# RWKV key factors: the sums one projection tile later, one square root ahead of the next eviction, and the spread to channels by sixteen 32-row products over four banks

## The chip, the cores and the metric

One core of one Trainium2 chip runs the whole program. The metric is device time in microseconds (us), the median of several executions. The engines are named as in the profile: PE (TensorE, matrix products), PEld (its weight loads), DVE (VectorE), ACT (ScalarE), POOL (GpSimd) and SP (SyncE, which here only issues transfers).

## The reference, cut to what matters

The program is a decoder trunk of two layers over 512 tokens with a model width of 1024. Each layer projects the normed tokens once (`proj = h @ w_in`), feeds three mixers with the parts of that product, projects back, attends to a memory and ends in a mixture of 32 experts. The change lies in one step of the RWKV mixer, which has 8 heads of 64 channels:

```python
kk = k * k_k.astype(f32).reshape(H, N)
kk = kk / jnp.maximum(jnp.sqrt(jnp.sum(kk * kk, axis=-1, keepdims=True)), 1e-12)
y = rwkv7_scan(r, decay, k, v, -kk, kk * a)
```

For every token and head the squares of the 64 channels of `kk` are summed, the reciprocal root of the sum is a factor, and all 64 channels are multiplied by it. There are 512 tokens by 8 heads of such factors in a layer.

## The kernel before, in words

Everything lies transposed: channels on the 128 partitions, tokens along the free dimension. The 512 RWKV channels of a quantity are four blocks c = 0 to 3 of 128 channels (two heads each). All data is f32, and a matrix product shows in the profile as two PE instructions (passes): eight products of a tile are 16 passes.

The stage around the change is the input projection (lines 708 to 1077). PE computes 19 tiles of 128 channels by 512 tokens, in the order `TILE_ORDER` (line 45), which is here called tile 0 to tile 18. A tile is eight products over the model width (line 1063), accumulated in one of the four PSUM banks B[0] to B[3] in turn. Before tile n PE waits until the bank's last tile has been evicted (`s_pad`). After each tile it looks in a table written by hand, `between` (line 1054), for other work to put in: `kk_sums` after tile 8, `kk_spread` after tile 10, `early_a` after tile 13. PE executes its instructions in this order, so whatever a `between` step waits for also holds up the next tile.

ACT evicts each tile (`evict(n)`, lines 774 to 784, copies at 782 or 784), DVE then mixes it with the tokens shifted by one (`shift(m)`, lines 871 to 880), where `shift(7)`, `shift(8)`, `shift(9)` belong to tiles 8, 9 and 10. Both engines also work in the order of the code.

The key factors go through all engines:

- DVE scales the keys into `X1` (line 906); ACT squares `X1` into `kk_sq` (line 830), between the evictions of tile 8 and tile 9.
- PE, `kk_sums` (line 998): `heads_summed` multiplies with `head_pick`, four blocks of 32 output rows for each c, so that rows 32i to 32i+31 of B[4], columns 0 to 127, hold the sums of head rows for the 128 tokens of token tile i. These are 16 products, 32 passes (line 287).
- DVE (lines 917 to 919), after `shift(8)`: floor at 1e-24 and reciprocal into `hf`, 128 x 128.
- POOL (line 762) has zeroed `kk_rs`, 128 x 512, after waiting for the sums. ACT (line 835), after `evict(10)`: `root_by_tile` takes the root of each 32-row band i of `hf` into columns 128i to 128i+127 of that band of `kk_rs` (four instructions, line 299), so that the other bands of these columns stay zero.
- PE, `kk_spread` (line 1003): `heads_given` multiplies the 128 x 128 matrix `head_give[:, c, :]` with `kk_rs`, one product of 512 columns for each c into B[4] to B[7] (line 293, eight passes in all).
- DVE (lines 921 to 923), after `shift(9)`: multiplies `X1[:, c, :]` with B[4 + c], each c as soon as its product is there. After tile 11 (`V_DONE`) it goes on with the decays and with A and B, which `early_a` needs (lines 925 to 938).

Each 32-row band of `head_give` holds the same pattern, written by POOL at the start of the stage (lines 755 to 760). The function `heads_given` and `root_by_tile` are used a second time later in the layer, in a stage that the change doesn't touch. After the stage come the recurrence, the output projection, the memory attention and the experts, whose weights SP loads into a ring of SBUF units as PE releases them (line 1979).

Of the kernel before, what the change touches and what calls it, by code (L numbers as in the profile page):

```python
# [9 lines left out]
ACT = mybir.ActivationFunctionType  # L10
# [3 lines left out]
P = 128  # L14
DEPTH, SEQ, D = 2, 512, 1024
NT = SEQ // P
KD = D // P
MEM = 256
RC = 4
# [52 lines left out]
def build(nc, xT_d, memT_d, pos_d, inv_d, colp_d, memcol_d, w_in_d, lora_d, gup_d, gup2_d, wuq_d, wukv_d, wsT_d,  # L72
          gb_d, w_out_d, wkv_d, wm_d, wr_d, br_d, we_d, out_d):
    ctx = ExitStack()
    with ctx:
# [15 lines left out]
        def sb(name, shape, dt=F32):  # L91
            return ctx.enter_context(nc.sbuf_tensor(name, shape, dt))
# [4 lines left out]
        def sem(name):  # L97
            stage.append(held[0].enter_context(nc.semaphore(name)))
            return stage[-1]
# [52 lines left out]
        B = [banks[:, i, :] for i in range(8)]  # L152
# [4 lines left out]
        ring = sb("ring", [P, 6, 4096])  # L157
# [47 lines left out]
        def in_chunks(ap):  # L205
            return ap.rearrange("p (q t) -> p q t", t=C)
# [74 lines left out]
        head_give = ring[:, 5, 1536:2048].rearrange("p (c n) -> p c n", c=RC)  # L281
# [9 lines left out]
        def heads_given(bank, c, src):  # L291

            return nc.tensor.matmul(bank[:, :], head_give[:, c, :], src, start=True, stop=True)

        def root_by_tile(eng, out, src):

            for i in range(NT):
                rows = slice(32 * i, 32 * i + 32)
                last = eng.activation(out[rows, i * P:(i + 1) * P], src[rows, :], ACT.Sqrt)
            return last  # L300
# [50 lines left out]
        def rows_landed(eng, done):  # L351
            eng.wait_ge(s_yo[0], 16 * (NE // 2) * done)
            eng.wait_ge(s_yo[1], 16 * (NE // 2) * done - 16)
            eng.wait_ge(s_yl, 32)
            if done == DEPTH:
                eng.wait_ge(s_yx, 32)
# [285 lines left out]
        for layer in range(DEPTH):  # L642
# [19 lines left out]
            for c in range(RC):  # L662
# [11 lines left out]
            s_b1, s_b2, s_b3 = sem("kk_squared"), sem("kk_summed"), sem("kk_floored")  # L674
            s_b4, s_b5 = sem("kk_root"), sem("lora_tanh")
            s_b6, s_b7, s_b8 = sem("kk_factors"), sem("kk_factors_spread"), sem("gate_tanh")
            s_kn = sem("kk_normed")
            hf, kk_rs = ring[:, 5, 2048:2048 + P], ring[:, 5, 3072:3584]
            s_hg, s_kz = sem("head_give_ready"), sem("kk_factors_zeroed")
            s_wp, s_ap, s_th, s_ta = sem("decay_lora"), sem("a_lora"), sem("decay_tanh"), sem("a_tanh")  # L680
            s_cr, s_ex, s_bp, s_bs = (sem("cum_ready"), sem("decay_exps"), sem("bonus_product"),
                                            sem("bonus_summed"))
# [8 lines left out]
            def flat(ap):  # L691
                return ap.rearrange("p c t -> p (c t)")
# [4 lines left out]
            NTILE = len(TILE_ORDER)  # L697
# [10 lines left out]
            with nc.Block() as block:  # L708
# [38 lines left out]
                @block.gpsimd  # L747
                def _(eng):
                    g = gch.on(eng)
                    if layer:  # L750
                        rows_landed(eng, layer)
                        combine_gather(eng, ys_d[0:NE * CAP, :])
                        scale_first(eng, layer)
                    g(eng.memset(shp[:, :, 0:1], 0.0))
                    g(eng.memset(head_give[:, :, :], 0.0))
                    for i in range(NT):
                        v = head_give[:, :, :].rearrange("p c (e n) -> p c e n", e=2)
                        g(eng.affine_select(out=v, in_=v, compare_op=ALU.not_equal, fill=1.0, base=-32 * i,
                                            pattern=[[-2, RC], [-1, 2], [0, RN]], channel_multiplier=1))
                    eng.sem_inc(s_hg, 1)  # L760
                    eng.wait_ge(s_bs, 1)
                    eng.memset(kk_rs, 0.0).then_inc(s_kz, 1)

                    eng.wait_ge(s_ai, 16)
                    g(eng.affine_select(out=l_blk, in_=a_blk, compare_op=ALU.is_gt, fill=0.0, base=0,
                                        pattern=[[1, 32], [-1, 32]], channel_multiplier=0))
                    eng.affine_select(out=l_blk, in_=l_blk, compare_op=ALU.not_equal, fill=1.0, base=0,
                                      pattern=[[1, 32], [-1, 32]], channel_multiplier=0).then_inc(s_bm, 1)

                @block.scalar  # L770
                def _(eng):
                    a = ach.on(eng)

                    def evict(n):
                        j = TILE_ORDER[n]
                        _, w, _, shifted = TILE[j]
                        eng.wait_ge(s_pj, n + 1)
                        if shifted:
                            m = sum(TILE[x][3] for x in TILE_ORDER[:n])
                            if m >= 2:  # L780
                                eng.wait_ge(s_sh, m - 1)
                            eng.activation(shp[:, m % 2, 1:SEQ + 1], B[n % 4][:, :], ACT.Copy).then_inc(s_pad, 1)  # L782
                        else:
                            eng.activation(dest[j][0:w, :], B[n % 4][0:w, :], ACT.Copy).then_inc(s_pad, 1)
# [29 lines left out]
                    for z in range(2):  # L814
                        for n in range(2):
                            c = 2 * z + n
# [12 lines left out]
                        eng.wait_ge(s_yz, 16)  # L829
                    eng.activation(flat(kk_sq), flat(X1), ACT.Square).then_inc(s_b2, 1)  # L830
                    evict(9)
                    evict(10)
                    eng.wait_ge(s_b3, 1)
                    eng.wait_ge(s_kz, 1)
                    root_by_tile(eng, kk_rs, hf).then_inc(s_b4, 1)
                    evict(11)
                    eng.wait_ge(s_cr, 1)
                    eng.activation(flat(X6), flat(X6), ACT.Exp).then_inc(s_ex, 1)
# [28 lines left out]
                def _(eng):  # L867
# [3 lines left out]
                    def shift(m):  # L871
                        n, j = order[m]
                        eng.wait_ge(s_pad, n + 1)
                        v(eng.tensor_tensor(shd[:, :], shp[:, m % 2, 0:SEQ], shp[:, m % 2, 1:SEQ + 1],  # L874
                                            ALU.subtract))
                        out = dest[j] if 4 <= j < 12 else in_chunks(dest[j])
                        eng.scalar_tensor_tensor(out=out, in0=in_chunks(shd[:, :]), scalar=col("mu", j),
                                                 in1=in_chunks(shp[:, m % 2, 1:SEQ + 1]), op0=ALU.mult,
                                                 op1=ALU.add).then_inc(s_sh, 1)
                        eng.wait_ge(s_sh, m + 1)  # L880
# [37 lines left out]
                    v(eng.tensor_scalar(hf, B[4][:, 0:P], 1e-24, None, ALU.max))  # L918
                    eng.reciprocal(hf, hf).then_inc(s_b3, 1)
                    shift(9)  # L920
                    for c in range(RC):
                        eng.wait_ge(s_b7, c + 1)
                        last = eng.tensor_tensor(X1[:, c, :], X1[:, c, :], B[4 + c][:, :], ALU.mult)
                    last.then_inc(s_kn, 1)
                    eng.wait_ge(s_pj, V_DONE)
# [53 lines left out]
                def _(eng):  # L979
                    def lora_pair(z):  # L980
                        if z == 0:
                            if not layer:
                                eng.wait_ge(s_kd, 2)
                            eng.wait_ge(s_par, 16 * NPAR * (layer + 1))
                            eng.wait_ge(s_sh, 1)
                            eng.wait_ge(s_b5, 1)
                        for n in range(2):
                            c, cols = 2 * z + n, slice((2 * z + n) * P, (2 * z + n + 1) * P)
                            if z:
                                eng.wait_ge(s_ta, n + 1)  # L990
                            nc.tensor.matmul(B[4 + 2 * n][:, :], lora_w[64:128, cols], lora[64:128, :],
                                             start=True, stop=True).then_inc(s_ap, 1)
                            if z:
                                eng.wait_ge(s_th, n + 1)
                            nc.tensor.matmul(B[5 + 2 * n][:, :], lora_w[0:64, cols], lora[0:64, :], start=True,
                                             stop=True).then_inc(s_wp, 1)
# [6 lines left out]
                    def kk_spread():  # L1003
                        eng.wait_ge(s_hg, 1)
                        eng.wait_ge(s_b4, 1)
                        for c in range(RC):
                            heads_given(B[4 + c], c, kk_rs).then_inc(s_b7, 1)

                    def early_a():
                        eng.wait_ge(s_ab, 2)  # L1010
# [40 lines left out]
                    else:  # L1051
                        nc.tensor.matmul(B[3][:, :], ones_mean[:, :], xsum, start=True, stop=True).then_inc(s_x0, 1)
                    first_products(2, KD).then_inc(s_pj, 1)
                    between = {5: lambda: lora_pair(0), 6: lambda: lora_pair(1), 8: kk_sums, 10: kk_spread, 13: early_a, NTILE + 1: bonus_sums}
                    for n, j in list(enumerate(TILE_ORDER))[1:]:
                        u0, w, unit, _s = TILE[j]
                        eng.wait_ge(s_win[unit], 16 * layer + 16)
# [2 lines left out]
                        for k in range(KD):  # L1060
                            if n == 1:
                                eng.wait_ge(s_h, k + 1)
                            last = nc.tensor.matmul(B[n % 4][0:w, :], ins_units[unit][:, k, u0:u0 + w], hT[:, k, :],  # L1063
                                                    start=k == 0, stop=k == KD - 1)
# [1929 lines left out]
```

## Time and profile before

| | |
|---|---|
| median of 3 runs | 1871.53 us (1870.42 to 1873.68) |
| the profiled execution: its own time | 1873.28 us |
| its span, first to last instruction | 1871.5 us |
| mean granted TensorE clock | 0.985 |
| PE busy | 1755.2 us, 94% of the span |
| DVE busy | 612.2 us, 33% |
| ACT busy | 386.5 us, 21% |
| POOL busy | 182.4 us, 10% |
| hardware DMA queue q1 | 475.45 MB, 62.2% of 16 engines' span |

The profile is of one execution. Starts are counted from the first instruction. "Busy" counts an engine's own instructions; the bracket behind a row of the timeline gives the idle time of that engine just before it and what ended it.
### The profile page before, as it was taken

What the parts mean: (1) busy time and instruction counts of PE and PEld (TensorE: products, weight loads), DVE (VectorE), ACT (ScalarE), POOL (GpSimd) and SP (SyncE); (2) the same over time, 40 slices, a digit from 0 to 9 for tenths busy, and PEclk for the clock granted to TensorE, in tenths of its full rate; (3) what the DMA queues carried; (4) which work ended last, traced back from release to release, by engine and by line L of the source; (5) the groups of instructions that cost most, each with busy time, mean ns of one, the idle gap of its engine ahead of it and who ended that gap; (6) DMA issues with size and microseconds to landing.
All of it is one profiled execution on the core that took longest, in us unless ns stands there. A gap on an engine that the chain in (4) does not pass through costs nothing. (4 is left out here: it accounts for less than half of the span.)

```text
span 1871.5 us, 26294 instructions
## 1 busy us (share of the span) xinstructions
PE 1755.2 (94%) x11146; PEld 866.8 (46%) x11146; DVE 612.2 (33%) x1163; ACT 386.5 (21%) x745; POOL 182.4 (10%) x223
## 2 busy tenths in 40 slices
PE   8989999999999999998699999999999999999985
PEld 6435765455444443433253467545554444333322
DVE  7347554236211111111243574612561111111102
ACT  3131364154000000000212324513510000000001
POOL 3000101004000000000300001000040000000001
PEclk9999999999999999999899999999999999999997
DMA  9502205135999999999850220243279999999996
GB/s 382 208 1 34 37 11 218 57 130 196 405 429 427 427 427 429 428 428 427 313 214 0 34 35 12 81 189 135 91 301 422 427 426 427 427 429 428 427 429 228
DMA packets 90489, 494.83 MB, mean 264 GB/s; under 512 B 45646, under 2 KB 50510, under 8 KB 62736
## 3 DMA queue, kind: packets, MB, share of 16 engines
q1 hardware_dynamic: 82672, 475.45, 62.2%
q0 software_dynamic: 7632, 17.74, 2.6%
q8 instruction: 80, 1.31, 0.3%
q14 instruction: 25, 0.20, 0.0%
q10 hardware_dynamic: 80, 0.13, 0.0%
HBM read 465.34 MB, written 36.18 MB: 268 GB/s over the span
## 5 line engine op out<-in xcount | busy, mean ns | idle before, releaser
L2203 PE MATMUL bank<-ring,hT 128*64 128x512 f32 x2048 | 465.8, 597 | 37.9 <-DMA ring<-in_we 31.7
L2203 PEld LDWEIGHTS bank<-ring,hT 128*64 128x64 f32 x2048 | 139.5, 136 | 313.9 <-issue 250.1
L1063 PE MATMUL bank<-hT,ring 128*128 128x512 f32 (+1 forms) x576 | 250.6, 595 | 0.0
L2211 PE MATMUL bank<-ring,arena 128*64 128x512 f32 x1040 | 236.7, 597 | 11.1 <-DMA ring<-in_we 9.1
L1063 PEld LDWEIGHTS bank<-hT,ring 128*128 128x128 f32 (+1 forms) x576 | 108.3, 189 | 138.8 <-issue 137.5
L2188 PE MATMUL bank<-shift_in,arena 128*128 128x256 bf16 (+1 forms) x1440 | 160.0, 268 | 0.0
L2188 PEld LDWEIGHTS bank<-shift_in,arena 128*128 128x128 bf16 x1440 | 129.9, 98 | 62.7 <-issue 48.7
L2256 DVE TENSOR_TENSOR hT<-bank,colp 128x512 f32<-128x512 f32 (+1 forms) x68 | 45.2, 668 | 340.0 <-PE bank L2188 328.5
L2592 ACT ACTIVATE arena<-bank 128x256 f32<-128x256 f32 x65 | 25.0, 384 | 605.1 <-PE bank L2174 605.1
L2221 POOL DMA_INDIRECT expert_rows<-arena,row_places x63 | 62.1, 986 | 847.3 <-DVE arena L2733 818.9
L2211 PEld LDWEIGHTS bank<-ring,arena 128*64 128x64 f32 x1040 | 71.0, 137 | 143.7 <-issue 126.2
L2733 DVE COPY arena<-bank 128x512 f32<-128x512 f32 x65 | 44.9, 691 | 252.6 <-PE bank L2211 252.2
L2369 PE MATMUL bank<-hT,ring 128*128 128x512 f32 x256 | 110.3, 593 | 2.2 <-PEq L1914 2.2
L2579 ACT ACTIVATE arena<-bank 128x512 f32<-128x512 f32 x65 | 38.9, 598 | 244.4 <-PE bank L2203 244.4
L2705 DVE TENSOR_TENSOR arena<-arena,bank 128x256 f32<-128x256 f32 x65 | 27.4, 421 | 187.6 <-ACT arena L2592 187.4
L2369 PEld LDWEIGHTS bank<-hT,ring 128*128 128x128 f32 x256 | 48.5, 190 | 62.9 <-issue 62.9
L2612 DVE TENSOR_TENSOR xT<-xT,bank 128x512 f32<-128x512 f32 x32 | 22.0, 687 | 138.7 <-PE bank L2369 105.8
L874 DVE TENSOR_TENSOR arena<-shift_in 128x512 f32<-128x512 f32 x30 | 22.1, 736 | 110.6 <-ACT shift_in L782 110.4
L782 ACT ACTIVATE shift_in<-bank 128x512 f32<-128x512 f32 x28 | 16.8, 599 | 178.6 <-PE bank L1063 178.6
L253 ACT ACTIVATE arena<-xT 128x512 f32<-128x512 f32 x32 | 20.2, 630 | 133.5 <-DVE xT L2612 133.5
L2174 PEld LDWEIGHTS bank<-ident,arena 128*128 128x128 f32 x260 | 28.0, 141 | 40.7 <-issue 40.6
L2174 PE MATMUL bank<-ident,arena 128*128 128x128 f32 x260 | 41.9, 284 | 0.0
(464 smaller groups left out, 1884.4 us busy)
## 6 DMA issues: line engine op xcount, KB each, us to landing
ring<-in_we SPq DMA_DIRECT2D x193, 2048.0 KB, 23.6
ring<-in_w_in SPq DMA_DIRECT2D x6, 2048.0 KB, 19.2
expert_rows<-ring SPq DMA_DIRECT2D x1, 8448.0 KB, 25.7
ring<-in_w_out SPq DMA_DIRECT2D x4, 2048.0 KB, 10.1
ring<-in_wm SPq DMA_DIRECT2D x2, 2048.0 KB, 7.3
ring<-in_w_in SPq DMA_DIRECT2D x2, 1920.0 KB, 16.5
ring<-in_w_in SPq DMA_DIRECT2D x2, 1664.0 KB, 27.0
ring<-in_w_in SPq DMA_DIRECT2D x2, 1152.0 KB, 28.7
```

The costliest lines, as they stand in the source:

```text
L1063: last = nc.tensor.matmul(B[n % 4][0:w, :], ins_units[unit][:, k, u0:u0 + w], hT[:, k, :], start=k == 0, stop=k == KD - 1)
L2174: last = nc.tensor.transpose(bank[:, j * P:(j + 1) * P], src[:, j * P:(j + 1) * P], ident[:, :])
L2188: last = nc.tensor.matmul(bank[:, o:o + w], parts[m][:, i, k * P:(k + 1) * P], selg[z][:, i, c0:c0 + w], start=m == 0 and i == 0, stop=m = ...
L2203: last = nc.tensor.matmul(bank[CAP * j:CAP * j + CAP, :], x[:, k, :], ahead_w[4 * j + k] if third else up_w(u, j, k), start=k == 0, stop=k ...
L2211: last = nc.tensor.matmul(bank[CAP * half:CAP * half + CAP, :], hid[u][:, m, :], down_w(slot, m, half), start=m == 0, stop=m == HM - 1)
L2221: eng.indirect_dma_start(out=ys_halves[0:2 * NE * CAP, :], out_offset=bass.IndirectOffsetOnAxis(ap=row_places[:, e:e + 1], axis=0), in_=ys ...
L2256: return eng.tensor_tensor(xgg[z][:, k0:k0 + n, c0:c0 + w], bank[:, 0:n * w].rearrange("p (k s) -> p k s", k=n), gain.unsqueeze(2).to_broa ...
L2369: last = nc.tensor.matmul(B[c % 4][:, :], w_out[:, k, c * P:(c + 1) * P], hT[:, k, :], start=k == 0, stop=k == KD - 1)
L2579: eng.activation(hr[w], b_up[w][:, :], ACT.Copy).then_inc(s_hr, 1)
L2592: eng.activation(sg[w], up_half(b_flip[w], 0), ACT.Silu).then_inc(s_sg, 1)
L2705: eng.tensor_tensor(hid[w], sg[w], up_half(b_flip[w], 1), ALU.mult).then_inc(s_hd, 1)
L2733: eng.tensor_copy(ysb[w], b_down[w][:, :]).then_inc(s_ys, 1)
```

## The change

`kk_sums` moves from after tile 8 to after tile 9. The root becomes one ACT instruction over `hf`, 128 x 128, in place, and moves ahead of `evict(10)`. `kk_rs`, its zeroing on POOL and their semaphore go. `kk_spread`, still after tile 10, becomes 16 products of 32 rows by 128 columns: in round r block c takes token tile i = (c + r) mod 4, so that a round's four products read four different 32-row bands and write four different banks, B[4] to B[7]. Before rounds 1 to 3 PE waits for the completion of its own products of the rounds before. DVE waits for all 16 before its first multiplication with the factors.

```diff
-            hf, kk_rs = ring[:, 5, 2048:2048 + P], ring[:, 5, 3072:3584]
-            s_hg, s_kz = sem("head_give_ready"), sem("kk_factors_zeroed")
+            hf = ring[:, 5, 2048:2048 + P]
+            s_hg = sem("head_give_ready")
@@ gpsimd
                     eng.sem_inc(s_hg, 1)
-                    eng.wait_ge(s_bs, 1)
-                    eng.memset(kk_rs, 0.0).then_inc(s_kz, 1)
-
                     eng.wait_ge(s_ai, 16)
@@ scalar
                     evict(9)
+                    eng.wait_ge(s_b3, 1)
+                    eng.activation(hf, hf, ACT.Sqrt).then_inc(s_b4, 1)
                     evict(10)
-                    eng.wait_ge(s_b3, 1)
-                    eng.wait_ge(s_kz, 1)
-                    root_by_tile(eng, kk_rs, hf).then_inc(s_b4, 1)
                     evict(11)
@@ vector
                     shift(9)
+                    eng.wait_ge(s_b7, RC * NT)
                     for c in range(RC):
-                        eng.wait_ge(s_b7, c + 1)
                         last = eng.tensor_tensor(X1[:, c, :], X1[:, c, :], B[4 + c][:, :], ALU.mult)
@@ tensor
                     def kk_spread():
                         eng.wait_ge(s_hg, 1)
                         eng.wait_ge(s_b4, 1)
-                        for c in range(RC):
-                            heads_given(B[4 + c], c, kk_rs).then_inc(s_b7, 1)
+                        for r in range(NT):
+                            if r:
+                                eng.wait_ge(s_b7, RC * r)
+                            for c in range(RC):
+                                i = (c + r) % NT
+                                rows = slice(32 * i, 32 * i + 32)
+                                nc.tensor.matmul(B[4 + c][:, i * P:(i + 1) * P], head_give[rows, c, :], hf[rows, :],
+                                                 start=True, stop=True).then_inc(s_b7, 1)
@@
-                    between = {5: lambda: lora_pair(0), 6: lambda: lora_pair(1), 8: kk_sums, 10: kk_spread, 13: early_a, NTILE + 1: bonus_sums}
+                    between = {5: lambda: lora_pair(0), 6: lambda: lora_pair(1), 9: kk_sums, 10: kk_spread, 13: early_a, NTILE + 1: bonus_sums}
```

## Rows read from the trace of the kernel before

**Rows 1.** The page: span, and busy time of each engine.

```profile
span 1871.5 us, 26294 instructions
...
PE 1755.2 (94%) x11146; PEld 866.8 (46%) x11146; DVE 612.2 (33%) x1163; ACT 386.5 (21%) x745; POOL 182.4 (10%) x223
```

**Rows 2.** Timeline, PE, layer 0: start us, length us, engine, line, operation, idle before.

```profile
80.92 13.97 PE L1063 MATMUL bank<-hT,ring 128*96 128x512 f32 x32
...
97.38 1.93 PE L287 MATMUL bank<-ring,head_pick 128*32 128x128 f32 x32 [2.49 <-ACT ring L830]
...
99.24 14.71 PE L1063 MATMUL bank<-hT,ring 128*128 128x512 f32 x32
...
117.30 5.37 PE L293 MATMUL bank<-ring 128*128 128x512 f32 x8 [3.35 <-ACT ring L299]
...
122.50 20.76 PE L1063 MATMUL bank<-hT,ring 128*128 128x512 f32 x48
```

**Rows 3.** The same timeline, PE, layer 1.

```profile
996.13 13.97 PE L1063 MATMUL bank<-hT,ring 128*96 128x512 f32 x32
...
1012.59 1.08 PE L287 MATMUL bank<-ring,head_pick 128*32 128x128 f32 x32 [2.48 <-ACT ring L830]
...
1013.60 14.00 PE L1063 MATMUL bank<-hT,ring 128*128 128x512 f32 x32
...
1030.95 3.67 PE L293 MATMUL bank<-ring 128*128 128x512 f32 x8 [3.35 <-ACT ring L299]
...
1034.46 20.76 PE L1063 MATMUL bank<-hT,ring 128*128 128x512 f32 x48
```

**Rows 4.** Stretches: busy us (instructions) of each engine, then granted clock, DMA share, GB/s.

```profile
80.92:122.50 41.58, 35.74 (x106) 15.49 (x105) 16.97 (x26) 8.36 (x13) 0.53 (x1) 0.92 0.00 1
996.13:1034.46 38.33, 32.49 (x106) 14.00 (x105) 16.98 (x26) 8.36 (x13) 0.53 (x1) 1.00 0.00 0
...
97.00:99.00 2.00, 1.62 (x32) 1.38 (x32) 0.50 (x5) 0.33 (x1) 0.00 (x0) 0.57 0.00 0
```

**Rows 5.** Timeline, matmuls on either side of a switch of array shape.

```profile
80.40 0.59 PE L995 MATMUL bank<-arena,lora_w 64*128 64x512 f32 x1
...
143.20 2.10 PE L1018 MATMUL bank<-ring 64*64 64x64 f32 x128
...
145.22 7.13 PE L1063 MATMUL bank<-hT,ring 128*128 128x512 f32 x16
```

**Rows 6.** Groups of instructions, 1012 to 1014.2 us: count, busy us, mean ns, idle before.

```profile
L287 PE MATMUL bank<-ring,head_pick 128*32 128x128 f32 x32 | 1.1, 276 | 2.5 <-ACT ring L830 2.5
```

**Rows 7.** Timeline, ACT, layer 0.

```profile
95.42 1.90 ACT L830 ACTIVATE ring<-ring 128x2048 f32<-128x2048 f32 x1
...
114.60 1.28 ACT L299 ACT_TABLE_LOAD   x1
...
115.89 1.26 ACT L299 ACTIVATE ring<-ring 32x128 f32<-32x128 f32 x4
...
130.19 1.28 ACT L838 ACT_TABLE_LOAD   x1
```

**Rows 8.** Timeline, DVE, layer 0.

```profile
109.33 0.29 DVE L918 TENSOR_SCALAR ring<-bank 128x128 f32<-128x128 f32 x1
...
109.66 0.95 DVE L919 RECIPROCAL ring<-ring 128x128 f32<-128x128 f32 x1
...
122.71 0.69 DVE L923 TENSOR_TENSOR ring<-ring,bank 128x512 f32<-128x512 f32 x1 [0.17 <-PE bank L293]
...
129.57 2.29 DVE L926 TENSOR_TENSOR ring<-ring 128x2048 f32<-128x2048 f32 x1 [6.18 <-PE bank L1063]
```

**Rows 9.** Waits from 80 to 200 us: waiter <- releaser, us, times, longest.

```profile
POOL ring L765 <- DMA ring<-decay_products: 59.5, 1, 59.5
```

**Rows 10.** Waits of the DMA-issuing queue of SP, whole span.

```profile
SPq L1979 <- PE bank L2203: 507.6, 120, 15.4
```

**Rows 11.** Chain that ended last: start us, us, what.

```profile
1585.21 25.96 DMA ring<-in_we
```

## The prediction

> **What bounds the kernel now.** I first read the page for the busiest engine: PE is busy for 1755.2 of 1871.5 us [rows 1]. An average says nothing of a stage, so next came PE's timeline around the changed step, in both layers [rows 2, 3]. To be seen there: passes of 512 columns follow each other without a gap, 48 of them in 20.76 us. With 0.59 us for the last one [rows 5], that is (20.76 - 0.59) / 47 = 0.429 us a pass and 6.86 us a tile. This line breaks only twice. After tile 8 PE stands for 2.49 us until ACT has squared the keys; after tile 10 it stands for 3.35 us until ACT has taken the root. Both are waits of the engine that sets the stage's time, for a chain that runs one tile too close behind it.
>
> The third view is the table of stretches [rows 4]. From the start of tile 7 to the start of tile 11 both layers do the same work, but layer 0 takes 41.58 us and layer 1 38.33 us. The granted clock says why: 0.92 against 1.00. In layer 0 it was down, 0.57 between 97 and 99 us, right behind the first stand, so it touched the lower level (1.2 GHz); layer 1 shows the same stands and no fall. DMA moves next to nothing in either (share 0.00).
>
> Last, does time won here arrive at the end? The chain that ended last runs from about 1585 us on through the transfer of expert weights [rows 11], but SP's queue issues those transfers when PE releases a ring unit [rows 10]. An earlier PE starts them earlier. So I take a gain in this stage for a gain of the whole.
>
> **The change part by part.** I add up the new stretch, tile 7 to the start of tile 11.
>
> *Sums moved behind tile 9.* ACT starts the square at 95.42 and takes 1.90 [rows 7], so it is done 2.6 us after tile 8, and tile 9 alone lasts 6.86. The wait goes. Tiles 7 and 8 take 13.81 (13.97 less the 0.16 by which a pass's end trails the next one's start), tile 9 takes 6.86, the 32 passes of the sums 1.01 (1012.59 to 1013.60) [rows 3]. Entering a tiled array shape costs about 0.10 more: 48 passes from 122.50 end their issue at 143.09, and the next line starts at 143.20 [rows 2, 5]. Tile 10 behind the sums: 6.98, since 32 passes took 13.84 there (1013.60 to 1013.60 + 14.00 - 0.16) and a plain tile 6.86; the first pass shows its weight load.
>
> *Root ahead of evict(10).* Before, DVE starts the floor behind `shift(8)` at 109.33 and ends the reciprocal at 110.61 [rows 8]. Tile 9 ended its last pass about 107.1 (113.95 less 6.86), so the reciprocal is ready 3.5 us after it. The sums are done 1.2 us after tile 9, earlier than `shift(8)`, so the 3.5 stands. ACT then takes one root of 128 x 128; its nearest rows are four of 32 x 128, 1.26 in all, 0.32 each, and I take 0.32, at most 1.26 [rows 7]. The table load of 1.28 stands in both versions; the one for the exponential at 130.19 began while DVE's L926 (129.57 to 131.86) was still to be waited for [rows 7, 8], so a load runs ahead of its wait. The root is ready 3.9 us after tile 9; even with the load behind the wait and the long root, 6.1. Tile 10 ends 1.1 + 6.98 = 8.1 after tile 9. PE finds it done: the 3.35 us wait goes. The new wait on ACT holds up only `evict(10)`, which can't start before tile 10 has ended anyway.
>
> *The spread.* Sixteen products are 32 passes, in four rounds of eight. No row has 32-row bands; the nearest are the sums, 32-column bands with 128 columns a pass: 32 passes in 1.08, one lasting 0.276 [rows 3, 6], so four run side by side and a slot of four takes (1.08 - 0.28) / 7 = 0.115. No row shows PE waiting for its own products. I build a round: second slot 0.11 after the first, then 0.28 until it has ended, 0.15 from a signal to PE's start (ACT's root ended at 117.15, PE began at 117.30 [rows 2, 7]) and 0.05 of exposed weight load: 0.59. Three such rounds and a last one of 0.3 make 2.05; entering the shape 0.10, leaving it a longer first pass of tile 11, 0.10 (16 passes in 7.13 at 145.22 instead of 7.03 [rows 5]). Lower bound: own waits cost nothing, the spread is like the sums, 1.01. Upper bound: the bands don't run side by side, 32 passes at a quarter of 0.429 (3.43), with three exposed ends of 0.28 - 0.11 + 0.05 + 0.15 = 0.37: 4.6. I take 2.05, built from the row with the same count and length of passes.
>
> By the Trainium skill ("TensorE: Matmul & The Clock Gate", section "The cost: per-tile semaphore tail") increments of concurrent products are carried out one after another, 25 + 4.7 x 4 + 26.3 x 4 = 149 ns for a group of four; as an addition to each of the six waited rounds that would be an estimate of 0.9 us against the change, and a sum of 17.0 where mine is 17.9. The traces show no row of it.
>
> *DVE, POOL.* DVE now waits for all 16 products, where before it took block by block and ended at 123.40, 6.18 us before it was needed [rows 8]. Now: `shift(9)` ends some 2.1 after tile 10, the spread 2.2, four multiplications of 0.69 make 5.0; tile 11 ends 2.2 + 6.9 = 9.1 after tile 10. Cover of 4.1 us; nothing is paid unless the spread grows by more. POOL's zeroing goes, and its next work waits 59.5 us for a transfer [rows 9]: nothing gained.
>
> **Sum.** 13.81 + 6.86 + 0.10 + 1.01 + 6.98 + 0.10 + 2.05 + 0.10 = 31.0 us. Layer 0 saves 41.6 - 31.0 = 10.6, of which 3.25 is the fallen clock (41.58 - 38.33); layer 1 saves 7.3. Together 17.9. The profiled execution took 1873.28 (span 1871.5), so it would take 1855.4; it lies 1.75 above the median, so I forecast 1853.6. With the bounds of the spread the saving is 20.0 or 12.8.
>
> **The rivals.**
>
> *The clock falls elsewhere.* The fall in layer 0 isn't tied to the stand alone, since layer 1 stood as long without one. If the changed kernel has a fall somewhere that this execution hadn't, or the runs behind the median had none here, the saving is 14.7: 1856.9. By the Trainium skill (same page, section "What's actually happening") the number of slow products at a start differs between runs of one kernel; that fits layers 0 and 1 differing. Chance 0.13.
>
> *The bands run one after another.* Then the spread is at its upper bound, the saving 12.8: 1858.7. For it: no row of this case has 32-row bands; against: the sums run four-wide. Chance 0.08.
>
> *The gain is hidden.* The transfers of expert weights end the chain [rows 11]; if their stream ran by its own time, all would be given back: 1871.5. Against it stand the issues that wait for PE [rows 10]. Chance 0.05.
>
> *Slower: PE's waits for itself.* Without the spread's 2.05 the saving would be 17.9 + 4.1 = 22.0; it is used up when the spread takes 11.0 a layer. That is (11.0 - 0.3 - 0.33) / 3 = 3.5 us for each of the three waits, where I take 0.48 behind the second slot. At 4.5 us a wait the spread is 3 x 4.61 + 0.3 = 14.1, twice that is 6.2 more than 22.0: 1877.7. For it: nothing shows such a wait. Against: ACT's signal reached PE in 0.15. Chance 0.04.
>
> **How the numbers follow.** The forecast has 0.70, its time is 1853.6. A change of 0.2%, 3.7 us, is about what a measurement of this kernel can tell. The range goes from 1850.0 (saving 20.0 from a run as low as 1870.4, rounded down) to 1860.5 (bands in turn, 1858.7, and most of the 2.15 by which runs lay above the median); it holds the forecast and the first two rivals. Faster by over 0.2%: 0.70 + 0.13 + 0.08 = 0.91; within: 0.05; slower: 0.04.
>
> **What the profile of the changed kernel would show.** Tile 9 starts directly behind tile 8; the line of sums behind tile 9 has no idle time, nor has the first product of the spread. From tile 7 to tile 11: 31 us in both layers at a granted clock of 1.00. ACT's root starts some 3.6 us after tile 9. Four rounds of eight passes about 0.6 us apart; if they are 1.2 apart the bands run in turn. DVE's line 926 still waits for tile 11. `early_a` starts without a wait. It would be wrong if a wait of PE for ACT stayed in front of the spread, if rounds lay microseconds apart, or if the stage ended 18 us sooner and the span did not.

## The result, and the profile after

The changed kernel takes 1856.03 us (median of 6 runs, 1854.12 to 1859.62) against 1873.29 us for the kernel before (6 runs beside it, 1870.42 to 1875.99): ratio 0.9914, 95% interval 0.9901 to 0.9928. It is faster by 17.3 us in the medians, by 13.5 to 18.5 with the interval; 17.9 were forecast, and 1856.03 lies inside the range. All medians, ratios and mean clocks of this document leave out two executions of 10105.81 and 5397.14 us, one of the kernel with one signal a round and one of the kernel before.

The page of the profiled execution, which itself took 1857.93 us, 1.9 above the median:

```profile
span 1856.2 us, 26380 instructions
...
PE 1745.5 (94%) x11194; PEld 863.8 (47%) x11194; DVE 612.6 (33%) x1163; ACT 383.7 (21%) x739; POOL 180.9 (10%) x221
```

PE's timeline around the step, first in layer 0, then in layer 1 (start us, length us). Line 1065 is the projection (1063 before), line 1008 the new spread:

```profile
81.02 20.84 PE L1065 MATMUL bank<-hT,ring 128*96 128x512 f32 x48
101.79 1.08 PE L287 MATMUL bank<-ring,head_pick 128*32 128x128 f32 x32
102.80 7.13 PE L1065 MATMUL bank<-hT,ring 128*128 128x512 f32 x16
109.86 0.50 PE L1008 MATMUL bank<-ring 32*128 32x128 f32 x8
110.53 0.50 PE L1008 MATMUL bank<-ring 32*128 32x128 f32 x8 [0.16 <-PE bank L1008]
111.20 0.51 PE L1008 MATMUL bank<-ring 32*128 32x128 f32 x8 [0.17 <-PE bank L1008]
111.87 0.50 PE L1008 MATMUL bank<-ring 32*128 32x128 f32 x8 [0.16 <-PE bank L1008]
112.30 20.87 PE L1065 MATMUL bank<-hT,ring 128*128 128x512 f32 x48
...
986.46 20.84 PE L1065 MATMUL bank<-hT,ring 128*96 128x512 f32 x48
1007.23 1.08 PE L287 MATMUL bank<-ring,head_pick 128*32 128x128 f32 x32
1008.24 7.13 PE L1065 MATMUL bank<-hT,ring 128*128 128x512 f32 x16
1015.30 0.51 PE L1008 MATMUL bank<-ring 32*128 32x128 f32 x8
...
1017.75 20.87 PE L1065 MATMUL bank<-hT,ring 128*128 128x512 f32 x48
```

Beside [rows 2, 3]: the three tiles 7, 8 and 9 are now one line of 48 passes, and the sums follow it without a bracket: no idle time. The same holds for the first round of the spread. The two stands of 2.49 and 3.35 us are gone in both layers. What is new are four rounds of eight passes 0.67 us apart, each but the first with 0.16 or 0.17 us in which PE waits for its own products (the release named in the bracket is PE itself). `early_a` starts at 133.10 without a wait, as forecast.

The same stretch in the table of stretches, with the granted clock, beside [rows 4]:

```profile
81.02:112.30 31.28, 30.79 (x130) 13.66 (x128) 14.95 (x23) 7.44 (x10) 0.00 (x0) 1.00 0.00 1
986.46:1017.75 31.29, 30.80 (x131) 13.67 (x129) 14.96 (x23) 7.43 (x10) 0.00 (x0) 1.00 0.00 1
```

The step from tile 7 to tile 11 takes 31.28 and 31.29 us where it took 41.58 and 38.33: 10.30 + 7.04 = 17.34 us. The medians differ by 17.26. The clock is at full speed in both layers. The first pass of tile 11 is longer behind the new spread, and that falls behind these stretches: tiles 11 to 13 take 20.80 us to the start of `early_a` (112.30 to 133.10), 20.70 before (122.50 to 143.20), in layer 1 20.79 and 20.69. From tile 7 to `early_a` the two layers together save 17.1 us.

ACT, layer 0, beside [rows 7]:

```profile
102.51 1.28 ACT L830 ACT_TABLE_LOAD   x1
105.42 0.31 ACT L830 ACTIVATE ring<-ring 128x128 f32<-128x128 f32 x1 [1.63 <-DVE ring L915]
109.97 0.60 ACT L779 ACTIVATE shift_in<-bank 128x512 f32<-128x512 f32 x1 [4.24 <-PE bank L1065]
```

The table load starts at 102.51, right behind the eviction, while the root itself waits for DVE until 105.42: the load does run ahead of the wait. The root ends 4.2 us before `evict(10)` at 109.97.

DVE, layer 0, beside [rows 8]:

```profile
104.11 0.29 DVE L914 TENSOR_SCALAR ring<-bank 128x128 f32<-128x128 f32 x1
104.44 0.95 DVE L915 RECIPROCAL ring<-ring 128x128 f32<-128x128 f32 x1
...
112.59 2.48 DVE L919 TENSOR_TENSOR ring<-ring,bank 128x512 f32<-128x512 f32 x4 [0.51 <-PE bank L1008]
119.47 2.29 DVE L922 TENSOR_TENSOR ring<-ring 128x2048 f32<-128x2048 f32 x1 [4.41 <-PE bank L1065]
```

The reciprocal ends at 105.39, 3.5 us after tile 9, as before. The four multiplications come as one block and end at 115.07; line 922 (926 before) still waits 4.4 us for tile 11, in place of 6.18.

**On the way to the end.** The spans of the two profiled executions differ by 15.3 us, not 17.3. Two lines each show how far ahead the later stages are, from the view of one source line in layer 0: durations in ns (min/median/max), then first and last start in us. The first is the projection behind the mixers (line 2369 before, 2371 after), the second the experts' first products. Before:

```profile
L2369 PE MATMUL bank<-hT,ring x128: 592/592/667, 317.1 to 371.7; 128*128 128x512 f32 x128
...
L2203 PE MATMUL bank<-ring,hT x1008: 592/592/644, 450.9 to 902.5; 128*64 128x512 f32 x168
```

After:

```profile
L2371 PE MATMUL bank<-hT,ring x128: 592/593/668, 306.5 to 361.1; 128*128 128x512 f32 x128
...
L2205 PE MATMUL bank<-ring,hT x1008: 592/593/644, 439.1 to 892.7; 128*64 128x512 f32 x168
```

The projection behind the mixers starts 10.6 us earlier, the first expert product 11.8, the last one 9.8. Layer 1 then adds its 7, and the span ends 15.3 ahead. So single executions differ by one or two microseconds in stages that the change doesn't touch. Whether the end of the program takes back part of what is won here is looked at over all the experiments, at the end of the next section.

### The profile page after: what moved, and what is told of

Read it like the earlier page. It is cut to its first block and busy times, and to the rows that moved or that the text cites. A ratio compares the mean times of both kernels' runs of the same rounds, so it can differ in the third digit from the quotient of the medians.

```text
span 1856.2 us, 26380 instructions
## 1 busy us (share of the span) xinstructions
PE 1745.5 (94%) x11194; PEld 863.8 (47%) x11194; DVE 612.6 (33%) x1163; ACT 383.7 (21%) x739; POOL 180.9 (10%) x221
## 5 line engine op out<-in xcount | busy, mean ns | idle before, releaser
L2213 PE MATMUL bank<-ring,arena 128*64 128x512 f32 x1040 | 236.8, 597 | 10.6 <-DMA ring<-in_we 8.5
L2614 DVE TENSOR_TENSOR xT<-xT,bank 128x512 f32<-128x512 f32 x32 | 22.0, 688 | 138.7 <-PE bank L2371 105.8
L870 DVE TENSOR_TENSOR arena<-shift_in 128x512 f32<-128x512 f32 x30 | 22.5, 750 | 103.9 <-ACT shift_in L779 103.7
```

The costliest lines, as they stand in the source:

```text
L2213: last = nc.tensor.matmul(bank[CAP * half:CAP * half + CAP, :], hid[u][:, m, :], down_w(slot, m, half), start=m == 0, stop=m == HM - 1)
```

## The experiments

All ratios are to the kernel before, run on the same chip beside them. A ratio is not quite the quotient of the two medians, so a difference in us can come out a little differently by either. The first four take the change apart.

**Sums later, alone.**

```diff
-                    between = {..., 8: kk_sums, 10: kk_spread, ...}
+                    between = {..., 9: kk_sums, 10: kk_spread, ...}
```

> The kernel before with the sums moved behind tile 9 and nothing else. Theory (the gain is PE's two stands, each removed by its own move): the 2.5 us stand in front of the sums goes, the 3.35 us stand in front of the spread stays. Tile 7 to tile 11: 35.7 us in layer 1 (38.33 before), 35.7 to 37.4 in layer 0 depending on whether the clock falls behind the stand that is left. Saving 2 x 2.6 us plus 0 to 3.3 of clock, ratio 0.9955 to 0.997. Rival (the move of the sums does nothing by itself, since the chain to the root only starts later): the stand in front of the spread grows by what the first one lost, stretch 38.3, ratio 1.000.

1866.66 us, ratio 0.9952 (0.9935 to 0.9968). The spread in layer 0 from PE's timeline, then the stretch from tile 7 to tile 11, layers 0 and 1:

```profile
113.30 3.67 PE L293 MATMUL bank<-ring 128*128 128x512 f32 x8 [3.35 <-ACT ring L299]
...
81.03:116.81 35.78, 32.42 (x106) 14.01 (x105) 16.99 (x26) 8.37 (x13) 0.53 (x1) 1.00 0.00 0
990.30:1027.78 37.48, 34.12 (x106) 14.60 (x105) 17.00 (x26) 8.38 (x13) 0.53 (x1) 0.95 0.00 0
```

35.78 us in layer 0, as the theory had it. The stand in front of the spread is still 3.35 us, so the rival, a longer stand there, falls. In layer 1 it is 37.48, because here the clock fell behind the stand that is left (granted clock 0.95 over the stretch), where the kernel before had its falls in layer 0. The same stand, 3.35 us in both layers, brought a fall in one and none in the other.

**Root ahead, alone.**

```diff
-                    evict(10)
                     eng.wait_ge(s_b3, 1)
                     eng.wait_ge(s_kz, 1)
                     root_by_tile(eng, kk_rs, hf).then_inc(s_b4, 1)
+                    evict(10)
```

> The kernel before with the four roots ahead of the eviction of tile 10 and nothing else. Theory: the 3.35 us stand in front of the spread goes, that in front of the sums stays. Tile 7 to tile 11: 34.8 us in layer 1, 34.8 to 36.4 in layer 0. Saving 2 x 3.5 us plus 0 to 3.3 of clock, ratio 0.9945 to 0.996. Rival (the table load and the wait on ACT come behind each other and the root is late for tile 10's end): a stand of 1 us or more is left in front of the spread.

1863.07 us, ratio 0.9927 (0.9909 to 0.9944). The spread in layer 0, then the stretches:

```profile
114.12 3.60 PE L293 MATMUL bank<-ring 128*128 128x512 f32 x8
...
81.18:117.56 36.38, 33.90 (x107) 15.02 (x106) 16.05 (x25) 8.36 (x13) 0.52 (x1) 0.95 0.00 1
993.45:1028.19 34.74, 32.26 (x107) 14.08 (x105) 16.04 (x25) 8.36 (x13) 0.52 (x1) 1.00 0.00 0
```

34.74 us in layer 1 (34.8 expected); layer 0 has 1.6 more and a clock of 0.95 behind the stand before the sums. No stand is left in front of the spread (no bracket behind its line), even with four roots instead of one. The root was never slow, it only stood behind an eviction that itself waits for PE.

**Both moves, dense spread** (the two diffs together).

> Both moves, with the spread still as four full products over the zeroed matrix: the change without its sixteen products. Theory: tile 7 to tile 11 takes 32.2 us in both layers (31.3 with the change), no clock fall; saving 2 x 6.1 plus 3.3 of clock = 15.4, that is about 1.6 to 1.8 us above the change, ratio 0.992. Rival (the sixteen products are what pays): the saving is under half of the change's 17.3, ratio above 0.9955.

1857.58 us, ratio 0.9895 (0.9875 to 0.9914).

```profile
80.97:113.15 32.18, 32.18 (x106) 14.08 (x105) 16.04 (x25) 8.37 (x13) 0.53 (x1) 1.00 0.00 1
987.26:1019.44 32.18, 32.18 (x106) 14.08 (x105) 16.04 (x25) 8.37 (x13) 0.53 (x1) 1.00 0.00 1
```

32.18 us in both layers at full clock: 9.40 + 6.15 = 15.55 of the change's 17.34 us in these stretches, without a single one of the sixteen products. The ratio is 0.9895, where 0.992 was expected. The rival, that the sixteen products are what pays, falls.

**Spread and single root, alone**: the change with the sums back behind tile 8 and the root behind `evict(10)`.

```diff
-                    eng.wait_ge(s_b3, 1)
-                    eng.activation(hf, hf, ACT.Sqrt).then_inc(s_b4, 1)
                     evict(10)
+                    eng.wait_ge(s_b3, 1)
+                    eng.activation(hf, hf, ACT.Sqrt).then_inc(s_b4, 1)
...
-                    between = {..., 9: kk_sums, ...}
+                    between = {..., 8: kk_sums, ...}
```

> The sixteen 32-row products and the single root alone, sums behind tile 8 and root behind the eviction of tile 10 as before. Theory: the spread takes 2.6 us with entering and leaving instead of 3.4, and one root is 0.95 shorter than four, which shortens the stand in front of it: 1.7 us a layer, saving 3.5 plus 0 to 3.3 of clock, ratio 0.9965 to 0.998; tile 7 to tile 11 about 36.6 us in layer 1. Rival (the sixteen products are what pays): ratio 0.9955 or less.

1870.75 us, ratio 0.9981 (0.9968 to 0.9995).

```profile
80.95:118.93 37.98, 32.63 (x131) 14.30 (x129) 14.96 (x23) 7.45 (x10) 0.00 (x0) 0.95 0.00 1
994.19:1030.73 36.54, 31.18 (x130) 13.81 (x128) 14.95 (x23) 7.45 (x10) 0.00 (x0) 0.99 0.00 0
...
118.93:124.00 5.07, 5.07 (x12) 2.27 (x9) 2.48 (x4) 0.00 (x0) 0.00 (x0) 0.68 0.00 0
1030.73:1036.00 5.27, 5.27 (x13) 2.37 (x10) 2.48 (x4) 0.00 (x0) 0.00 (x0) 0.73 0.02 3
```

36.54 us in layer 1, 1.8 below the kernel before, about half of it from the shorter stand behind one root. Small, as the theory says, and the stands stay. The last two rows show what the stretches don't: right behind the spread, which follows a stand of 2.40 us here, the granted clock was 0.68 in layer 0 and 0.73 in layer 1, and tiles 11 to 13 took 22.40 and 22.18 us in place of 20.70 and 20.69. So of the 1.8 us won in layer 1 all but 0.3 were lost again to the clock.

**The four beside each other.** The ratios of the first three came out lower than expected: 0.9952 against 0.9955 to 0.997, 0.9927 against 0.9945 to 0.996 (here the whole interval lies below the expectation), 0.9895 against 0.992; that of the fourth, 0.9981, lies at the upper edge of 0.9965 to 0.998. By the medians the four save 8.6, 12.2, 17.7 and 4.5 us, by the traces, from tile 7 to `early_a` in both layers, 6.6, 8.8, 15.5 and 2.2. All four savings are 2.0 to 3.4 us above those of the traces. The kernel before had a median of 1875.28 us on that chip, 2.0 above the 1873.28 of its profiled execution, from which the traces' savings are taken. That accounts for most of the surplus; the rest was not traced.

The next four ask for mechanisms.

**Filler in the stands**: the kernel before with unused products, so that PE is busy while it would wait.

```diff
                     def kk_sums():
+                        eng.wait_ge(s_th, 4)
+                        keep_busy(B[7], 3, 4 * P)
...
                     def kk_spread():
+                        keep_busy(B[7], 3, 4 * P)
```

> The kernel before with three unused full products (2.57 us) put into each of PE's two stands, on a bank that is free; the path is otherwise as before. Theory (in layer 0 part of the loss was the fallen clock behind the stands): no fall in either layer, tile 7 to tile 11 takes 38.3 us in layer 0 as in layer 1 (41.58 before), saving up to 3.3 us, ratio 0.998 to 0.9995. Rival (the fall comes by itself and the stand has no part in it): layer 0 stays at 39.9 us or more.

1870.53 us, ratio 0.9980 (0.9966 to 0.9995).

```profile
80.59:118.95 38.36, 37.58 (x119) 16.29 (x118) 16.98 (x26) 8.37 (x13) 0.53 (x1) 1.00 0.00 1
993.95:1032.30 38.35, 37.57 (x119) 16.28 (x117) 16.98 (x26) 8.36 (x13) 0.53 (x1) 1.00 0.00 0
```

38.36 us in layer 0, the same as layer 1, against 41.58: the path is as long as before, and the 3.2 us of the fallen clock are gone. So part of what the change gives in layer 0 is clock. In the kernel before it fell twice there, behind the first stand [rows 4] and again behind the second, under the eight passes of the spread (the same table, kernel before):

```profile
117.30:122.50 5.20, 5.20 (x8) 2.17 (x9) 2.03 (x3) 0.00 (x0) 0.00 (x0) 0.67 0.02 3
```

One profiled execution alone couldn't show that filling the stands is what kept it up, since the kernel before had falls in only one of its layers. All runs together bear it out: the mean granted clock of ten runs with filler is 0.988, that of the kernel before beside them 0.985 (22 runs).

**Spread twice**: the rounds done eight times instead of four.

```diff
-                        for r in range(NT):
+                        for r in range(2 * NT):
...
-                    eng.wait_ge(s_b7, RC * NT)
+                    eng.wait_ge(s_b7, 2 * RC * NT)
```

> The change with its four rounds done twice. Theory (PE sets the end of this stage and the stage the end of the whole): four more rounds of 0.67 us, 2.7 us a layer, so 5.4 us more than the change, ratio to the kernel before 0.994. Rival (other work covers PE here): the stretch grows by 2.7 us but the time by less than 2.

1865.56 us, ratio 0.9953 (0.9934 to 0.9972): 0.39% of the kernel before, 7.3 us, above the change's ratio, where 5.4 were expected. Timeline of layer 0 (first round, last round, tile 11 and on), then the stretch behind the spread:

```profile
109.83 0.50 PE L1008 MATMUL bank<-ring 32*128 32x128 f32 x8
...
114.51 0.50 PE L1008 MATMUL bank<-ring 32*128 32x128 f32 x8 [0.17 <-PE bank L1008]
114.94 22.56 PE L1065 MATMUL bank<-hT,ring 128*128 128x512 f32 x48
...
114.94:120.00 5.06, 5.06 (x12) 2.22 (x9) 2.48 (x4) 0.00 (x0) 0.00 (x0) 0.66 0.00 0
```

The rounds cost what they should, 0.67 us each. But behind eight of them the clock fell: 48 passes take 22.56 us in place of 20.87, and the granted clock is 0.66 between 114.94 and 120 us. That is 1.7 us on top of 5.4, close to the 7.3; the intervals of the two ratios are wider than those 1.7, so it is the trace that shows it. Layer 1 had no fall (1.00 over the 5 us behind the rounds). No stand is longer than 0.17 us here, so thin work on PE can cost the clock too. The forecast hadn't that.

**One band in a round**: the four products of a round on the same 32 rows.

```diff
-                                i = (c + r) % NT
+                                i = r
```

> The change with the four products of a round on the same 32-row band, so that nothing in a round can run side by side. Theory (the rotation of bands makes a round of eight passes as short as two passes): eight passes of 0.107 to 0.115 one behind the other instead of two slots, so a round of 1.3 us instead of 0.67, the spread 5.2 us instead of 2.5, 5.3 us more than the change in all. Rival (a round's 0.67 us is all latency and waiting, and the bands never ran side by side): rounds stay at 0.7 to 0.8 us.

1866.64 us, ratio 0.9952 (0.9936 to 0.9967): by the ratios 7.1 us above the change, where 5.3 were expected. Layer 0:

```profile
109.76 4.79 PE L1008 MATMUL bank<-ring 32*128 32x128 f32 x32
114.48 22.56 PE L1065 MATMUL bank<-hT,ring 128*128 128x512 f32 x48
```

The spread takes 4.7 us instead of 2.4 (109.76 to 114.48), rounds are 1.2 us apart. The rotation over bands does let four products run side by side. Here too the clock fell behind the spread, in both layers: in layer 1 it was already down before the spread ended (0.86 over its 5.40 us) and at 0.50 over the 5 us behind.

**One signal a round.**

```diff
-                                eng.wait_ge(s_b7, RC * r)
+                                eng.wait_ge(s_b7, r)
                             for c in range(RC):
...
-                                nc.tensor.matmul(...).then_inc(s_b7, 1)
+                                last = nc.tensor.matmul(...)
+                            last.then_inc(s_b7, 1)
...
-                    eng.wait_ge(s_b7, RC * NT)
+                    eng.wait_ge(s_b7, NT)
```

> The change with one signal in each round, on the fourth product, instead of four. By the Trainium skill (TensorE: Matmul & The Clock Gate, The cost: per-tile semaphore tail) increments are carried out one after another, so three fewer in a round should save about 0.08 us a round. Theory (the round's wait is the drain and the way of one signal): rounds become 0.6 to 0.67 us apart, the time stays within 0.7 us of the change. Rival (the signals queue up and are most of the wait): rounds fall to 0.5 us or below.

1855.23 us, ratio 0.9897 (0.9869 to 0.9925). Layer 0:

```profile
109.87 2.28 PE L1008 MATMUL bank<-ring 32*128 32x128 f32 x32
112.08 20.87 PE L1066 MATMUL bank<-hT,ring 128*128 128x512 f32 x48
```

The spread takes 2.21 us (109.87 to 112.08) against 2.44 in the change, 0.23 less for the three waited rounds, 0.08 a round. That is the figure that the Trainium skill leads to ("TensorE: Matmul & The Clock Gate", section "The cost: per-tile semaphore tail": about 26 ns for each increment, three fewer). The trace agrees. The rounds start at 109.87, 110.46, 111.05 and 111.64: a waited round is 0.59 us. Within a round both versions look alike: the second four passes start 0.21 us after the first four and end 0.50 after them. From there to the next round it is 0.09 us with one signal and 0.17 with four. (Ends of products are modelled in these traces, starts are not.) So most of a round is its own passes, and three of the four signals cost 0.08 us of it.

**Extra dense work in front of the spread.**

```diff
                     def kk_spread():
+                        keep_busy(B[7], 6, 4 * P)
```

> The change with six unused full products (12 passes of 0.429 us, 5.15 us) in front of each spread, so that PE is lengthened by dense work, without the thin rounds that doubling the spread added. Theory (PE sets the stage and the stage the end; what doubling the spread cost beyond its 5.4 us was a fallen clock behind it): 10.3 us more than the change, to within 1.5. Rival (part of any lengthening here is covered later, by the transfers of expert weights): under 8 us more.

1866.51 us, ratio 0.9972 (0.9959 to 0.9984); the change on the same chip had 0.9917. By the ratios that is 10.3 us more, by the medians 8.6.

```profile
80.35 20.84 PE L1066 MATMUL bank<-hT,ring 128*96 128x512 f32 x48
...
109.11 5.31 PE L231 MATMUL bank<-mask,ident 128*128 128x512 f32 x12
...
116.79 20.87 PE L1066 MATMUL bank<-hT,ring 128*128 128x512 f32 x48
...
992.77 20.84 PE L1066 MATMUL bank<-hT,ring 128*96 128x512 f32 x48
...
1029.20 20.87 PE L1066 MATMUL bank<-hT,ring 128*128 128x512 f32 x48
```

Both stretches are 36.4 us instead of 31.3. Tile 7 of layer 1 starts at 992.77 against 986.46 in the change (987.66 in its second profiled execution), 6.3 and 5.1 us later: the 5.15 added in layer 0 are still there a layer later. No clock fell behind the dense work (20.87 us for the 48 passes). The two ways to count give 8.6 and 10.3 us, and by the intervals of the ratios 10.3 is good to some 4 us: the theory's 10.3 fits, and the rival's "under 8" is not excluded by the times alone. The spans of the profiled executions differ by only 7.4 and 6.8 us. The table below settles more.

**The three versions side by side**, five rounds each: one signal, the change, both moves with the dense spread.

> One signal a round again, beside the change itself and the dense spread on the same chip. Theory: the spread is 0.23 us shorter in each layer than the change's (2.21 against 2.44 in the first look), 0.5 us in all, below what the times can tell.

> The change itself once more. Theory: 17 us below the kernel before, ratio 0.990 to 0.992; tile 7 to tile 11 in 31.3 us in both layers.

> Both moves with the dense spread once more. Theory: 1.8 us above the change (32.2 against 31.3 us for tile 7 to tile 11, twice), so between 0 and 3 us. Rival (the thin rounds cost the clock later what they save): at or below the change.

| version | median us | ratio (95%) | tile 7 to tile 11, both layers |
|---|---|---|---|
| one signal a round | 1853.98 | 0.9906 (0.9885 to 0.9927) | 31.05 |
| the change | 1857.89 | 0.9917 (0.9897 to 0.9937) | 31.28 |
| both moves, dense spread | 1856.12 | 0.9917 (0.9898 to 0.9935) | 32.19 |

The change repeats its result. The stretch of the dense spread is 0.9 us longer in each layer (0.8 with the longer first pass of tile 11), yet its whole time can't be told from the change's: its median is 1.8 us lower, where up to 3 higher were expected, and beside the first four experiments its ratio was even 0.9895. That is the outcome that the rival named, but its mechanism doesn't show: the granted clock is 1.00 around the spread in both kernels, and over all runs it is 0.987 with the dense spread and 0.988 with the change. So the sixteen products shorten PE's work where they stand, but no gain in the whole is shown for them, and what hides the 1.6 us stays open; it is less than single executions differ by. One signal a round has the lowest median of the three and the shortest stretch; the intervals overlap, so it is the version to keep, not one shown to be faster than the change.

**All kernels in one table.** The two stretches from tile 7 to `early_a`, one in each layer, are added up; what is left of the profiled execution's span is the rest of the program, which no experiment touches. The last column is the mean granted clock over all runs of a kernel.

| kernel | both stretches, us | rest of the span, us | clock, all runs |
|---|---|---|---|
| before | 121.3 | 1750.2 | 0.985 (51 runs) |
| spread and single root, alone | 119.1 | 1750.4 | 0.985 (10) |
| filler in the stands | 118.1 | 1753.3 | 0.988 (10) |
| sums later, alone | 114.7 | 1750.0 | 0.986 (4) |
| extra dense work | 114.5 | 1749.1 | 0.987 (10) |
| one band in a round | 113.7 | 1755.4 | 0.985 (10) |
| root ahead, alone | 112.5 | 1752.1 | 0.988 (4) |
| spread twice | 111.2 | 1750.5 | 0.985 (7) |
| both moves, dense spread | 105.8, 105.8 | 1750.0, 1748.1 | 0.988 (4), 0.987 (6) |
| the change | 104.2, 104.2 | 1752.0, 1752.6 | 0.988 (12) |
| one signal a round | 103.7, 103.7 | 1750.0, 1748.5 | 0.988 (4), 0.988 (5) |

The rest takes 1748 to 1755 us whether the stretches are 104 or 121 us long, and it doesn't grow as they shrink. So what is won in this stage reaches the end of the program, to within the spread of single executions; a stream of transfers that ran by its own time would have kept the span as it was. The last column says that the fallen clock is no accident of one profiled execution: it is 0.985 to 0.986 in the kernels that keep the stand in front of the spread and in the two with longer thin work, and 0.987 to 0.988 in all others (also with the root alone moved, though a stand in front of the sums is left there). Within 22 runs of the kernel before, 0.001 of mean clock goes with about 1.3 us of time (a straight line through them), so the 0.003 between before and the change are worth some 3 to 4 us, an estimate that fits the 3.25 of the trace.

## Why the prediction was right

- **Sums behind tile 9:** no stand, 1.01 us for the sums (101.79 to 102.80), 0.10 on either side. As forecast; alone it gives 2.6 us at full clock (layer 0: 38.36 with filler, 35.78 with the sums moved).
- **Root ahead:** ready at 105.73, 3.9 us after tile 9 (its last pass ended at 101.86), 3.9 forecast, with 4.1 us to spare before PE wants it. One root of 128 x 128 takes 0.31 us.
- **The spread:** the one term that was mis-sized. 2.05 us were taken, 2.44 measured. A waited round is 0.67 us and not 0.59, and the last one takes 0.43 until tile 11 starts, not 0.30. Inside the round the second four passes start 0.21 us after the first and not 0.11, as the sums had suggested, so the round's passes end at 0.50 and not at 0.39; behind them come 0.17 us and not 0.20 (0.15 for the signal and 0.05 of exposed weight load, a term that stood in no row and that no run shows by itself). That the kernel with one signal has a round of exactly 0.59 is luck: 0.11 too little for the passes and 0.11 too much for the wait. The rule of the Trainium skill that the prediction put beside its sum ("TensorE: Matmul & The Clock Gate", section "The cost: per-tile semaphore tail", an estimate of 149 ns for four signals) is no addition to my 0.20; it is close to the whole 0.17 us that the trace shows between the end of a round and the next. In all the stretches came out 0.28 us longer than the 31.0 of the sum. That sum also counted the 0.10 of tile 11's first pass, which falls behind the stretch; like for like it is 0.38 a layer, and 17.1 us saved in the place of 17.9.
- **The clock:** 3.25 us were counted for layer 0, and the filler returned 3.22 of them (41.58 to 38.36). The prediction read the fall behind the first stand only. A second one followed the stand in front of the spread: a clock of 0.67, and eight passes in 5.37 us where layer 1 took 3.67. Each cost some 1.6 us, and the sum had both, since it took the whole difference of the layers. That the fall isn't tied to a layer was part of a rival and holds too: it sat in layer 1 when only the sums had moved. The rival's saving of 14.7 us lies within 13.5 to 18.5, so the total alone doesn't rule it out; the filler and the mean clocks of all runs speak against it.
- **DVE:** the cover of 4.1 us was 4.4.
- **The time itself:** 1856.03 us is 2.4 above the 1853.6. 1.8 of it is the base: the kernel before had 1873.29 beside the change and not 1871.53. The saving is what was forecast well, and the total can't tell 17.9 from 17.1.
- **The rivals:** bands one after another would have been 1.2 us a round, which is what they take on one band (4.7 us in all, 4.6 by the prediction's upper bound). PE's wait for itself is 0.46 us from the start of the second four passes to the next round, 0.17 of it idle, where 0.48 was taken and 3.5 would have used up the gain. That the transfers of expert weights hide the gain is not borne out: the rest of the program takes as long with the shortest stretches as with the longest.
- **What the forecast lacked:** the thin rounds can cost the clock themselves. With four rounds it stayed at full speed in both profiled executions of the change; with eight, or on one band, or behind a stand of 2.40 us, it fell.

## What to carry to other kernels

When an in-order engine is the bound, look for its few stands in an otherwise gapless line and ask by how much the chain behind each is late; moving the consumer one work unit later, or the producer ahead of an instruction that waits for that same engine, removed nearly all of the loss here (15.5 of 17.1 us), without less work done. Packing small products to save PE time was worth little where each group must end before the next starts: 0.8 us a layer in PE's line, and nothing that the whole time could show. One completion signal a group was enough. Fill, or remove, stands of TensorE of some microseconds: behind stands of 2.4 to 3.4 us even the dense work ran at the lower clock for a while here, in some layers and not in others, at about 1.6 us each.

## What the hardware showed beyond that

- Behind 5.1 us of rounds with at most 0.17 us of idle time between them, the granted clock was 0.66 over the next 5 us in layer 0, and at full speed in layer 1. Behind 2.4 us of the same rounds no fall was seen in either layer of the two profiled executions of the change; with a stand of 2.40 us in front of them it was 0.68 and 0.73 over the next 5 us.
- A stand of 3.35 us in front of the spread brought a fall in layer 0 in the kernel before, in layer 1 with the sums moved, and none in the other layer of each.
- Eight passes of 128 columns on four 32-row bands have a period of 0.59 us with one signal and 0.67 with four when PE waits for them; on one band 1.2. The passes themselves end 0.50 us after the start.
